# Retention heads issued in two overlapped halves, and key/value tiles of the attention preparation issued by generators of their own

## What is computed

```python
def retention_chunks(q, k, v, log_g, state):      # CHUNK = 128, 4 heads of 128; run forwards and, flipped, backwards
    def step(s, blk):
        qb, kb, vb = blk
        scores = jnp.einsum('bhid,bhjd->bhij', qb, kb) * decay_in
        o = jnp.einsum('bhij,bhjd->bhid', scores, vb) + jnp.einsum('bhid,bhde->bhie', qb, s) * q_decay
        s = s * chunk_decay + jnp.einsum('bhjd,bhje->bhde', kb * k_decay, vb)
        return s, o

y_ret = head_norm(o_ret, ret_g) * jax.nn.silu(p[5])

def attn_mixer(hx, hc, ang, in_w, out_w, q_norm, k_norm, ctx_out):
    q, k, v, g = jnp.split(hx @ in_w, cuts, axis=-1)                       # 8 query heads, 2 key/value heads of 128
    q = rope_2d(rmsnorm(q.reshape(B, L, N_HEADS, HEAD_DIM), q_norm), ang)
    k = rope_2d(rmsnorm(k.reshape(B, L, N_KV, HEAD_DIM), k_norm), ang)
    ...
    yx = (jax.nn.silu(g) * o) @ out_w
```

## Time and profile before

| | us |
|---|---|
| median of 6 runs (lowest to highest) | 8725.08 (8712.02 to 8787.93) |
| the profiled execution | 8714.87 |
| its span, first to last instruction of the slowest core (core 6) | 8713.3 |
| spans of the 8 cores | 8686.3 to 8713.3 |
| busy PE / DVE / ACT / POOL | 5650.1 / 3169.7 / 2873.5 / 2701.5 |

### The profile page before, as it was taken

How to read it: one execution, slowest core, us unless ns; L and a number is a source line. 1 busy time by engine, 2 the same in 40 slices (tenths; PEclk the granted TensorE clock), 3 DMA queues, 4 the chain that set the end, 5 groups by cost and what they waited for, 6 DMA issues and landing times.

```text
span 8713.3 us, 89978 instructions; the slowest of 8 cores (8686.3 to 8713.3 us)
## 1 busy us (share of the span) xinstructions
PE 5650.1 (65%) x26453; PEld 2645.4 (30%) x26924; DVE 3169.7 (36%) x4237; ACT 2873.5 (33%) x5290; POOL 2701.5 (31%) x2254
## 2 busy tenths in 40 slices
PE   3496877852222497878865434444444699999998
PEld 0243433421111143333322212222222344444443
DVE  0334252524444303212212245555555233333333
ACT  0324243311111001000000023333333677777776
POOL 0132221233343104324424445554555111111111
PEclk8697988975555598989987767777777899999999
DMA  3422212121121113444456611111111221112111
GB/s 117 101 73 70 77 65 87 54 85 49 54 60 49 49 61 128 154 148 137 144 164 209 197 40 40 54 40 54 51 45 45 73 72 54 67 49 72 59 54 39
DMA packets 322988, 706.06 MB, mean 81 GB/s; under 512 B 136240, under 2 KB 200145, under 8 KB 307099
## 3 DMA queue, kind: packets, MB, share of 16 engines
q1 hardware_dynamic: 254160, 473.72, 16.7%
q0 software_dynamic: 68352, 226.54, 7.7%
HBM read 509.20 MB, written 208.79 MB: 82 GB/s over the span
## 4 chain that ended last, share of the span: by engine, by line
PE 48%; DMA 13%; issue 13%; POOL 11%; DVE 7%; ACT 6%; SPq 1%; DVEq 0%; POOLq 0%; ACTq 0%
PE p_pb L489 5%; PE p_pb L896 5%; PE p_pb L1313 5%; PE p_pb L1323 5%; PE p_pb L1279 4%; PE p_pb L561 4%; PE p_pb L907 3%; PE p_pb L546 3%; DMA s_uw<-u_fm 3%; PE p_pb L829 3%; PE p_pb L1204 3%; DMA x<-s_tm 2%; PE p_pb L1058 2%; POOL s_sqt L960 1%; DMA s_yTs<-yT 1%
## 5 line engine op out<-in xcount | busy, mean ns | idle before, releaser
L1281 ACT ACTIVATE s_PTh<-p_pb 128x512 bf16<-128x512 f32 x2304 | 1354.3, 596 | 391.8 <-PE p_pb L1279 297.5
L1313 PE MATMUL p_pb<-s_PTh,s_av 128*128 128x512 bf16 x2254 | 858.5, 381 | 88.3 <-ACT s_PTh L1281 77.2
L1279 PE MATMUL p_pb<-s_aqT,s_akT 128*128 128x512 bf16 x2257 | 854.0, 381 | 38.8 <-DMA s_aqT<-aqT 36.3
L1323 PE MATMUL p_pb<-s_PTh,s_ones 128*128 128x512 bf16 x2262 | 861.4, 381 | 27.3 <-POOL s_mhalf L1153 23.7
L1291 DVE RECIPROCAL s_rden<-p_pb 128x512 f32<-128x512 f32 x128 | 429.2, 3353 | 460.2 <-PE p_pb L1323 460.2
L907 PE MATMUL p_pb<-s_Fib,s_Y 128*128 128x512 bf16 x2008 | 474.2, 397 | 127.2 <-DMA s_Fib<-k_finv 98.2
L489 PE MATMUL p_pb<-s_hxT,s_inw 128*128 128x512 bf16 (+1 forms) x2504 | 515.3, 366 | 17.3 <-DMA s_inw<-er_in_w 12.5
L1294 POOL TENSOR_TENSOR s_ogT<-s_tmo,s_asg 128x512 bf16<-128x512 f32 x128 | 147.6, 1153 | 1004.5 <-DVE s_tmo L1293 1004.5
L896 PE MATMUL p_pb<-s_utm,s_Fb 128*128 128x512 bf16 x2008 | 448.5, 384 | 15.6 <-DMA s_Fb<-k_ffwd 13.5
L948 PE MATMUL p_pb<-s_ow,s_yTs 128*128 128x512 bf16 x1129 | 267.2, 397 | 209.8 <-DMA s_yTs<-yT 123.9
L1101 PE MATMUL p_pb<-s_ident_bf,s_qr 128*128 128x128 bf16 x512 | 64.7, 306 | 516.1 <-POOL s_qr L996 515.1
(11 more groups left out here) (231 smaller groups left out, 10117.9 us busy)
## 6 DMA issues: line engine op xcount, KB each, us to landing
s_Fb<-k_ffwd SPq DMA_DIRECT2D x40, 2048.0 KB
s_xt<-x SPq DMA_DIRECT2D x128, 512.0 KB
s_Fib<-k_finv SPq DMA_DIRECT2D x64, 1024.0 KB
x<-s_tm POOLq DMA_DIRECT2D x72, 512.0 KB, 4.0
s_xtl<-x SPq DMA_DIRECT2D x72, 512.0 KB
s_xta<-x SPq DMA_DIRECT2D x64, 512.0 KB
out<-s_x POOLq DMA_DIRECT2D x64, 512.0 KB, 3.0
...
```

Of the source, the lines that this page charges most:

```text
L1279: sy.op("pe", lambda e: e.matmul(ps_[:], kT[:, h // 4, kt * 128:(kt + 1) * 128], qT[:, h, :], start=True, stop=True), reads=[t_kT, t_qT], ...
L1281: sy.op("act", lambda e: e.activation(out=PTh[hb][:, kt, :], in_=ps_[:], func=AF.Exp, scale=ks), reads=[tps], writes=[t_PTh[hb][kt]])
L1313: sy.op("pe", lambda e: e.matmul(po[:], v[:, kt, g * 128:(g + 1) * 128], PTh[hb][:, kt, :], start=(kt == 0), stop=(kt == NT - 1)), reads=[ ...
L1323: sy.op("pe", lambda e: e.matmul(pd[:], ones[:], PTh[hb][:, kt, :], start=(kt == KD), stop=(kt == NT - 1)), reads=[t_PTh[hb][kt], t_c], wr ...
```

## The change

In `phase2` a head's code is split into two generators, `head_front` and `head_back`, whose content is that of the two halves above. `head_front(0)` runs alone; after that `head_back(i)` and `head_front(i+1)` are interleaved, with the back's step first. Between one recurrence step and the next, the front now yields. In `l1_prep` the keys and values leave `x_tile` and become four generators `x_tile_kv`, which wait (in recording order, not on the chip) until their tile is normalized, and which have rings of temporaries of their own (`sqk`, `lstk`, `rtk`). Several `yield`s between a PE group and the ACT copy of its result are gone, in `norm_tile_g`, `kv_tile`, `x_tile` and `gate_fm`. The instructions are the same in number and size. Ring depths of the old rings don't change.

```diff
@@ norm_tile_g
-    yield
     mf = cx.modFM[l]
@@ phase2
-        for b in range(NB):
-            for h in range(4):
...
+        def head_front(b, h, C):
...
+            yield
+            sy.op("pool", lambda e: e.tensor_tensor(out=qf[:], in0=q3, in1=qd[:, h, :].unsqueeze(1).to_broadcast([128, NT, 128]), op=ALU.mult),
+                  reads=[t_q, t_c], writes=[t_qf])
+            yield
...
+            for idx in range(NC_ - 1):
+                pt, tp = nb(pD, "d")
                 for di in range(2):
...
+                yield
+            for di in range(2):
+                sy.op("act", lambda e: e.activation(out=Sbf[di][0][:], in_=S32[di][0][:], func=AF.Copy), reads=[S32[di][1]], writes=[Sbf[di][1]])
...
+            yield
...
+            for pair in ((0, 4), (8, 12), (16,)):
+                gens = [group(g0) for g0 in pair]
+                while gens:
+                    for g in list(gens):
+                        try:
+                            next(g)
+                        except StopIteration:
+                            gens.remove(g)
                     yield
...
+        hl = [(b, h) for b in range(NB) for h in range(4)]
+        Cs = [dict() for _ in hl]
+        interleave([head_front(hl[0][0], hl[0][1], Cs[0])])
+        for i in range(len(hl)):
+            gens = [head_back(Cs[i])]
+            if i + 1 < len(hl):
+                gens.append(head_front(hl[i + 1][0], hl[i + 1][1], Cs[i + 1]))
+            interleave(gens)
@@ l1_prep, kv_tile
-                yield
                 kvf, t_kvf = kvf_r.next()
...
-                yield from head_norm_rope(cx, kvf, t_kvf, 2, gk, t_c, (rcos, rsin), (tt - 2) if tt >= 2 else None, kr, t_kr, tmpset())
+                yield from head_norm_rope(cx, kvf, t_kvf, 2, gk, t_c, (rcos, rsin), (tt - 2) if tt >= 2 else None, kr, t_kr, tmpset_k())
@@ l1_prep, x_tile
+                flags[i] = True
...
-                yield from kv_tile(tt, hxq, t_hxq_i, i * 128)
+
+            def x_tile_kv(qg, i, hxq, t_hxq_i, flags):
+                while not flags[i]:
+                    yield
+                yield from kv_tile(2 + qg * 4 + i, hxq, t_hxq_i, i * 128)
@@ l1_prep
-                interleave([x_tile(qg, i, hxq, t_hxq[i], qTst, t_qTst) for i in range(4)] + gate_gens)
+                flags = [False] * 4
+                interleave([x_tile(qg, i, hxq, t_hxq[i], qTst, t_qTst, flags) for i in range(4)]
+                           + [x_tile_kv(qg, i, hxq, t_hxq[i], flags) for i in range(4)] + gate_gens)
```

More of the change, by code:

```diff
@@ L987, in head_norm_rope @@
     ra = sq[:, 0:nh * 64].rearrange("p (h m) -> p h m", m=64)
-    rb = sq[:, 512:512 + nh * 64].rearrange("p (h m) -> p h m", m=64)
+    rb = sq[:, nh * 64:2 * nh * 64].rearrange("p (h m) -> p h m", m=64)
     sy.op("dve", lambda e: e.tensor_tensor(out=ra, in0=x0, in1=cb, op=ALU.mult), reads=[t_src, t_c, t_st], writes=[t_sq])
@@ L1031, in l1_prep @@
         rt_r = [Ring(sy, ph, f"rt{i}", 4, [128, 8, 64], F32) for i in range(2)]
+        sqk_r = Ring(sy, ph, "sqk", 4, [128, 256], F32)
+        stk_r = Ring(sy, ph, "lstk", 8, [128, 24], F32)
+        rtk_r = [Ring(sy, ph, f"rtk{i}", 4, [128, 2, 64], F32) for i in range(2)]
         kTst_r = Ring(sy, ph, "kTst", 1, [128, 2, TOK], BF16)
@@ L1048, in tmpset, with tmpset_k @@
             return (sq, t_sq, st, t_st, rs[0][0], rs[1][0], [r[1] for r in rs])
+        def tmpset_k():
+            sq, t_sq = sqk_r.next()
+            st, t_st = stk_r.next()
+            rs = [r.next() for r in rtk_r]
+            return (sq, t_sq, st, t_st, rs[0][0], rs[1][0], [r[1] for r in rs])
         gate_gens = []
@@ L1081, in ctx_tile, with x_tile @@
                 yield from kv_tile(tt, hxa, t_hxa, 0)
-            def x_tile(qg, i, hxq, t_hxq_i, qTst, t_qTst):
+            def x_tile(qg, i, hxq, t_hxq_i, qTst, t_qTst, flags):
                 tt = 2 + qg * 4 + i
@@ L1092, in x_tile @@
                                                        start=(k == 0), stop=(k == 7)), reads=[t_hxq_i, t_inw], writes=[tp])
+                    sy.op("act", lambda e: e.activation(out=qf[:, half * 512:(half + 1) * 512], in_=pt[:], func=AF.Copy), reads=[tp], writes=[t_qf])
                     yield
-                    sy.op("act", lambda e: e.activation(out=qf[:, half * 512:(half + 1) * 512], in_=pt[:], func=AF.Copy), reads=[tp], writes=[t_qf])
-                yield
                 qr, t_qr = qr_r.next()
```

193 lines of the change are left out of this document (96 added, 97 removed).

## The result

The changed kernel takes 8682.24 us (median of 10 runs, 8671.19 to 8818.17), the kernel before 8728.22 us in the same comparison (20 runs). The ratio is 0.9941, with a 95% interval of 0.9912 to 0.9971: about 0.6% faster. The forecast was 8628, 1.0% faster, within 8520 to 8750. The profiled execution took 8678.43 us, of which core 3, the slowest, spans 8676.8. Stages are those of one traced core.

What follows compares the result with a forecast made beforehand. No engine is near full; both stretches are bound by chains of short operations handed from engine to engine. From 8714.9, −141 in `phase2` and +54 in `l1_prep` give 8628 us, range 8520 to 8750.

Steps and rivals of the forecast that it cites:

- T to M: `phase2`: from the end of a head's short-group scores (T) to a later head's first recurrence step (M), 23.8 us.
- M to T: `phase2`: from a head's first recurrence step to the next end of short-group scores, 23.6 + 8.65 us.
- recurrence and Sbf: `phase2`: recurrence steps and Sbf copies among the back's work add 8.65 us: half the steps, all of Sbf.
- end, from the last M to the last store: `phase2`: the last back runs alone, 77.4 us in all where 50.5 stood before, 26.9 more.
- DVE's scaling of k and the mean negations: `phase2`: now ahead of the first recurrence step, they can hold it; 0.8 us added, an estimate.
- Rival 3: `phase2`: recurrence fully exposed, 8684 us; if the scaling of k also comes late, 8744; chance 0.15.
- the store ahead of the squares: `l1_prep`, steady group: POOL's queries' squares stand behind a gate's store and begin 8.0 us later.
- the keys' passes: `l1_prep`, rope stage: keys' passes on POOL (8.4) and DVE (3.9) add up to +12.3 us a steady group.
- 7.0 of PE's projections: `l1_prep`, steady group: four kv projections on PE ahead of the queries' second halves add 7.0 us.
- context term: `l1_prep`: the context tiles, which have no rope, were put at 0 change.
- Rival 1: `l1_prep`: the keys' passes hide in waits of the rope stage, 8432 us; chance 0.08.
- Rival 2: `l1_prep`: POOL's blocks of keys' passes starve DVE, 14.2 us a group, slower at 8855 us; chance 0.09.

Runs made afterwards that it cites:

- e7: Changed kernel with each gate's store recorded one step later, behind the queries' squares on POOL; its dies took 8528 and 8562 us.
- e6: Changed kernel without the keys' scale by k_norm and their rope for the image tiles (computes other keys); its dies took 8523 to 8571 us.

## Why the prediction came out as it did

The measured time lies in the range and moved the way that was forecast, by 46 us where about 100 were forecast. The chain was the one that was forecast; one term of it was mis-sized in `phase2`, and in `l1_prep` the sum is in part luck.

**The path through `phase2`: right but for one term.** The forecast period was 23.8 + 32.25 = 56.1 us; the mean of the 14 is 59.5. The period below, with kf held, is 60.2.

| us | forecast | measured |
|---|---|---|
| first period | 20.1 | 20.1 |
| T to M (2067.61 to 2095.98) | 23.8 | 28.4 |
| M to T (2035.74 to 2067.61) | 32.25 | 31.9 |
| of it recurrence and Sbf | 8.65 | about 8.3 |
| end, from the last M to the last store | 77.4 | 75.3 |

M to T splits into 0.53, 11.16, 9.15, 10.61 and 0.42 from row to row above, against 0.6, 8.49, 5.37, 8.66 and 0.42 of the sum. So recurrence and Sbf cost together what was taken for them; how it divides between the two was not measured. (By its own terms, half of 16 × 0.52 and 4.1, the forecast's 8.65 would be 8.3.) **The step that failed is the 0.8 us for "DVE's scaling of k and the mean negations".** It measured 28.4 − 23.0 = 5.4: M comes 5.9 us after POOL's last product, where the sum had 0.3 + 0.8, because the held scaling keeps masks, sums and negations behind it (1.27 of masks, the PE groups, two sums, the negations). Over the 14 periods the mean of 59.5 makes 14 × 3.4 = 48 us more than forecast, of which the end gives back 2.1; with 0.9 from the rounded period and end of before this is the 47 by which the stage misses its forecast. I priced the scaling from the row that it had in the middle of the chain, where POOL stood idle, and looked at its load alone. Two rows of before showed the other price, at the start of head 0, where the scalings first stand beside products; the third row is the price in a later head:

```profile
1881.34 5.22 DVE L651 TENSOR_SCALAR s_kf<-s_kh,s_kd 128x2304 bf16<-128x2304 bf16 x1
1886.48 5.12 DVE L653 TENSOR_SCALAR s_kb<-s_kh,s_kd 128x2304 bf16<-128x2304 bf16 x1
...
2008.60 0.81 DVE L651 TENSOR_SCALAR s_kf<-s_kh,s_kd 128x2304 bf16<-128x2304 bf16 x1
```

A step that is moved takes on what runs beside it in its new place. In the old order k was loaded a head ahead, and kf ran as soon as DVE was free, 3.8 us ahead of qf (2008.60 and 2012.37). In the new one its load, issued at T, lands just as POOL comes to qf (2076.59 and 2076.44), and in most heads the product wins. The Trainium skill, SBUF — State Buffer, "Who interferes with whom", lists tensor_scalar among the operations that can exclude GpSimd's, beside the ones with two inputs in SBUF; I had weighed its sentence for `l1_prep` alone. The trace agrees, with 14.10 us for kf beside the products and 0.82 without.

**Rival 3** gave the right size, 8684, for the wrong reason: it put the period's excess into a fully exposed recurrence (+3.75), and at M to T none of it is seen. Its second half, DVE holding the masks behind a late scaling, is what happened; but of the time from DVE's wait to kf's end the load is 3.51 us and POOL's products are 13.3.

**`l1_prep`: the sum right, in part by luck.** A steady group went from 100.9 to 104.7 (mean of 11 of the 12), +3.8 where +4.5 was forecast. Inside it the squares begin 42.87 us behind the Squares instead of 27.54, +15.3 (forecast 15.6 = 7.0 + 0.6 + 8.0); the rope stage grew by 11.4 (forecast 12.3); what follows the stage to the next Squares is 4.95 (forecast 2.5 + 4.6 = 7.1) instead of 2.5 and the tail. Two terms have an experiment of their own and are shown: the store ahead of the squares (forecast 8.0; in e7 the squares came 6.6 earlier and the group was 9.7 shorter) and the keys' passes (forecast 12.3; 10.3 in e6). The 7.0 of PE's projections was not tested alone. Outside the steady groups two errors cancel, which is luck: three context stages cost +19.7 together, forecast 0, and the four first groups gained 17.1, forecast 0. The context term failed because I counted ACT's and POOL's order and not that a store, too, holds its buffer.

**Rival 1** (keys hidden) is out by e6. **Rival 2** had its mechanism right, since DVE is held for 12 us at a stretch in the rope stage, but not its price: POOL, which holds it, goes on with its own work, and pays only the 4.73 us at the end, in a stage that grew no more than the plain sum of both engines' passes. The prediction said that POOL needs no result of DVE there; the wait shows that its last sum does wait for DVE's subtraction, which writes the same tile, as it did before the change (1.20 us ahead of the keys' sum at 5349.20).
